# Eight matmuls of the ones matrix with itself at TensorE's beginning

## What is computed

```python
def rms_norm(x, g):
    y = x * lax.rsqrt(jnp.mean(x * x, axis=-1, keepdims=True) + RMS_EPS)
    return y * g
def swiglu(x, w1, w3, w2):
    return (jax.nn.silu(x @ w1) * (x @ w3)) @ w2

x = x + 0.5 * swiglu(rms_norm(x, g_ffn1), w1_ffn1, w3_ffn1, w2_ffn1)
...
x = x + concat(attention, gated_spatial_mix) @ w_out + b_out
x = x + 0.5 * swiglu(rms_norm(x, g_ffn2), w1_ffn2, w3_ffn2, w2_ffn2)
x = x + sigmoid(rms_norm(x, g_ple) @ w_ple_gate) * (ple @ w_ple_proj)
```

## Time and profile before

| | us |
|---|---|
| median of 3 executions | 979.13 |
| all of them | 979.13, 980.75, 979.12 |
| the profiled execution | 978.99 |
| its span, from the first instruction to the last | 977.2 |
| mean granted TensorE clock | 0.998 of full |
| busy: PE / DVE / ACT / POOL | 960.1 / 673.4 / 456.0 / 251.7 |

### The profile page before, as it was taken

One profiled execution on the slowest core, in us unless ns is written; L12 is line 12 of the kernel. 1 busy time (PEld: TensorE's weight loads), 2 busy tenths in 40 slices (PEclk: granted clock), 3 DMA queues, 4 the chain that ended last, 5 costly groups with the idle time before them and its releaser, 6 DMA issues.

```text
span 977.2 us, 19305 instructions
## 1 busy us (share of the span) xinstructions
PE 960.1 (98%) x7949; PEld 946.1 (97%) x7949; DVE 673.4 (69%) x1071; ACT 456.0 (47%) x746; POOL 251.7 (26%) x146
## 2 busy tenths in 40 slices
PE   7999999999999999999999999999999999999997
PEld 7999999999999999998899999999999999999997
DVE  6999567757668564467765399857766758855476
ACT  7555335533534444665444455534543443635243
POOL 0212211211111226422308411301221211114621
PEclk9999999999999999999999999999999999999999
DMA  8931524152143327321124693253324325235202
GB/s 240 172 88 55 161 66 119 46 163 78 53 131 108 98 76 206 82 65 45 44 60 125 129 173 97 64 143 97 98 81 115 98 61 144 66 98 163 88 22 88
DMA packets 190098, 100.33 MB, mean 103 GB/s; under 512 B 12986, under 2 KB 187412, under 8 KB 189996
## 3 DMA queue, kind: packets, MB, share of 16 engines
q1 hardware_dynamic: 176612, 90.27, 32.5%
q0 software_dynamic: 9360, 4.72, 3.9%
q10 hardware_dynamic: 4040, 4.12, 1.4%
HBM read 96.54 MB, written 3.59 MB: 102 GB/s over the span
## 4 chain that ended last, share of the span: by engine, by line
PE 86%; DVE 9%; issue 2%; ACT 1%; DMA 1%; SPq 0%; DVEq 0%
PE ps L1778 46%; PE ps L1858 34%; PE ps L2205 2%; PE ps L1814 1%; DVE w_lo L1350 1%; DMA x_rows<-in_x_prompt_dram 1%; PE ps L2079 1%; DVE xo_lo L1316 1%; PE ps L2108 1%; DVE w_lo L1476 0%; DVE tt L1275 0%; DVE w_raw L1339 0%; DVE tt L1494 0%; PE ps L1803 0%; DVE xo_raw L1293 0%
## 5 line engine op out<-in xcount | busy, mean ns | idle before, releaser
L1858 PE MATMUL ps<-xo_hi,w_hi 128*128 128x260 f32 x1008 | 284.2, 282 | 1.2 <-DVE ab L1373 1.2
L1858 PE MATMUL ps<-xo_lo,w_hi 128*128 128x260 f32 x1008 | 284.7, 282 | 0.0
L1858 PE MATMUL ps<-xo_hi,w_lo 128*128 128x260 f32 x1008 | 284.4, 282 | 0.0
L1778 PE MATMUL ps<-h_hi,w_hi 128*128 128x260 f32 x960 | 195.3, 285 | 1.0 <-issue 0.6
L1778 PE MATMUL ps<-h_hi,w_lo 128*128 128x260 f32 x960 | 193.0, 282 | 0.0
L1778 PE MATMUL ps<-h_lo,w_hi 128*128 128x260 f32 x960 | 192.9, 282 | 0.0
L1858 PEld LDWEIGHTS ps<-xo_hi,w_hi 128*128 128x128 f32 x1008 | 189.6, 188 | 1.3 <-issue 1.3
L1858 PEld LDWEIGHTS ps<-xo_hi,w_lo 128*128 128x128 f32 x1008 | 189.8, 188 | 0.0
L1858 PEld LDWEIGHTS ps<-xo_lo,w_hi 128*128 128x128 f32 x1008 | 189.7, 188 | 0.0
L1778 PEld LDWEIGHTS ps<-h_hi,w_hi 128*128 128x128 f32 x960 | 147.5, 188 | 2.5 <-issue 1.3
L1778 PEld LDWEIGHTS ps<-h_lo,w_hi 128*128 128x128 f32 x960 | 148.1, 188 | 0.0
(11 more groups left out here) (280 smaller groups left out, 1449.1 us busy)
## 6 DMA issues: line engine op xcount, KB each, us to landing
w_raw<-in_w_ffn_dram SPq DMA_DIRECT2D x88, 256.0 KB, 3.1
w_a<-in_w_ffn_dram SPq DMA_DIRECT2D x36, 512.0 KB, 4.8
w_raw<-in_w_ffn_dram SPq DMA_DIRECT2D x48, 384.0 KB, 3.3
w_raw<-in_w_ffn_dram SPq DMA_DIRECT2D x16, 512.0 KB, 6.0
w_raw<-in_w_in_dram SPq DMA_DIRECT2D x10, 512.0 KB, 4.0
w_lo<-in_w_ffn_dram POOLq DMA_DIRECT2D x9, 512.0 KB, 7.4
w_raw<-in_w_ple_gate_dram SPq DMA_DIRECT2D x8, 512.0 KB, 3.6
x_rows<-in_x_prompt_dram SPq DMA_DIRECT2D x8, 256.0 KB, 6.1
```

The source lines that it names most:

```text
L1778: ins = pe.matmul(ps[:, bank + step * h, 0:HALF], w[:, c, w0:w0 + P], m_[:, sk, h * HALF:(h + 1) * HALF], start=(first and n == 0), stop=( ...
L1858: ins = pe.matmul(ps[:, b, 0:Q], w[:, c, k * P:(k + 1) * P], m_[:, op, k, :], start=(first and k == 0 and n == 0), stop=(k == 3 and n == 2 ...
```

## The change

Between the wait for the constants and the wait for the gains, TensorE multiplies `ones` by `ones` eight times, into the first 128 columns of bank 0. Nothing waits for these matmuls and nothing reads their result; the first up tile begins this bank anew. No semaphore is added.

```diff
             pe.wait_ge(consts_ready, 4)
+            for _ in range(8):
+                pe.matmul(ps[:, 0, 0:P], ones[:], ones[:], start=True, stop=True)
             pe.wait_ge(gain_in, 16)
             pe.transpose(ps[:, 7, 0:KD], rows[0:KD, :], ident[0:KD, 0:KD]).then_inc(cols_turned, 1)
             pe.wait_ge(x_in[NB], 16)
```

## The result

The changed kernel takes 982.43 us (median of 22 executions, 980.32 to 983.87), the kernel before 979.76 (22 executions, 978.70 to 981.46): a ratio of 1.0022, 95% interval 1.0016 to 1.0028. Forecast was 979.0, within 978.2 to 980.4. So it is slower, by about as much as the bound of 0.2% that the prediction set. The profiled execution takes 982.27, its span is 980.2. Three executions among all runs (1036, 1436 and 1561 us, at a lower granted clock) are left out of every comparison.

What follows compares the result with a forecast made beforehand. TensorE was taken to bound the kernel (busy 98% of the span), except in the first 20 us, where the chain runs over other engines. 978.99 - 0.1 = 978.9, set at 979.0 for the runs' median; range 978.2 to 980.4.

Steps and rivals of the forecast that it cites:

- Cost of the added work and what it delays: TensorE's start: 16 records take 3.34 us, until 5.14; samples' transposes 0.54 later, hidden by waits and DVE's slack.
- The rise of the clock: First 14 us: TensorE reaches full clock about 6.8 instead of 13.6 us, within the left halves' transposes; gain 0.1 us.
- rival 1: At the start the clock stays at half until 10 or 13.6 us: 979.4 us, chance 0.20.
- if the 32 transposes all take 421: Sign of being wrong: all transposes of `x_rows` at the start still take 421 ns, the half-clock time.
- That a faster TensorE gains next to nothing there: Right halves' transposes save 1.5 us on TensorE, but DVE's and ACT's streams let only 0.1 through.
- The longer wait for `w_lo` at 20 us: TensorE's first up tile starts about 0.9 us sooner, so it waits longer than 0.43 us for the second's `w_lo`.
- a gain of 0.1 us: Copy of slice 0 comes at about 8.75 instead of 8.85 us, and 0.1 passes through the ACT stream.
- the second up tile begins at 20.05 instead of 20.15: Last step of the sum, near 20 us: TensorE's second up tile starts 0.1 us earlier, taken off 978.99.
- Rival 3: Half-clock stretch from 484.6 to 488.1 us goes away, saving 1.7: 977.4 us, chance 0.08; under 977.2, chance 0.03.
- a sign of being wrong: The prediction listed itself as wrong if the half-clock stretch at 485 us is gone.
- Rival 4: TensorE idles from 8.4 to 10.3 us, clock falls again, first up tile slow: 980.4, chance 0.05; over 981.1, chance 0.03.
- That the clock rises behind transposes alone: At 13.6 us the trace shows the clock rising after nothing but transposes, against a skill rule; the sum follows the trace.

Runs made afterwards that it cites:

- e1: The changed kernel run once more, with no further edit: 981.88 us, 1.0020 to the kernel before.
- e9: Kernel before plus two 128x512 ones matmuls at TensorE's beginning instead of the change's eight, so 8 instructions more: 980.24 us, 1.0006.
- e5: Changed kernel with 32 instructions fewer at TensorE's end, transposes there replaced by six fast matmuls, so the old program length: 980.30 us, 0.9999.
- e3: Kernel before with the eight ones matmuls at the end of TensorE's program instead of its beginning: 981.66 us, 1.0020.
- e2: Kernel before, unedited, loaded as a second program: 980.77 us, 1.0010.
- e6: Kernel before with transposes at TensorE's end replaced by six fast matmuls, 32 instructions fewer, no early ones matmuls: 979.93 us, 0.9995.

## Why the prediction was wrong

- *Cost of the added work and what it delays*: right in kind, short in size. The 16 records took 3.78 us where 3.34 were reckoned, so the gains' transpose came at 5.48 and not at 5.14. The left halves began at 6.23 (forecast 6.22) all the same, by luck: the clock rose earlier than chosen, and the samples' transposes took 0.69 us instead of 1.02. The cost stayed hidden behind loads and DVE's slack: copy of slice 0 at 8.74 (forecast 8.75), copy of slice 4 without idle time, second up tile at 20.03 (forecast 20.05).
- *The rise of the clock*: right in kind in the change's profile, full before the first transpose of `x_rows`, where I had chosen 6.8. In e1's profile of the same kernel *rival 1* (chance 0.20) came true instead, and with it the sign "if the 32 transposes all take 421". That a faster TensorE gains next to nothing there, since DVE's and ACT's streams set the end: right. The longer wait for `w_lo` at 20 us didn't come (0.43 before and now); TensorE spent the time inside the tile (0.21 of it waiting for `h_lo` at 15.36). The kernels with the early work and no slow loads agree: e9 1.0006 and e5 0.9999, each with an interval around no difference. They can't confirm a gain of 0.1 us.
- **The step that failed is the one that wasn't there.** The sum ended at 20 us: "the second up tile begins at 20.05 instead of 20.15", and the 957 us behind it were taken over unchanged. The prediction counted the 16 records by their run time and never as 32 more instructions of a program. What happened is that 384 KB loads take 0.3 us longer, which five places in the program can't hide (1.7 us). It isn't the early work: e3 has the eight at the far end and the same loss, e5 has them at the beginning and the old length and no loss.
- *Rival 3* spoke of the fall at 484.6 going away, at a gain of 1.7. It did go away in the change's profile, which was a sign of being wrong, and nothing was gained: the wait for `mix_lo` behind it absorbed it (1.6 against 2.8 us), and behind the longer idle time the clock fell, at full price. It fell there in all four profiles with a wait of 2.8 us and in none of the eleven with 1.3 to 1.6; that the idle time is the cause isn't shown. The rival's price was taken from the lost work alone, without asking what ends last behind it. The form changes without a change of program: the kernel before has the short fall at 484 in one profile and the long one in the other (e2), and the change has the one at 510 and, in e1, the short one near 486. So it is at least in part spread among executions; whether the change makes a dear form more frequent stays open.
- *Rival 4*, my only slower one, didn't occur: TensorE was idle for 2.02 us ahead of 10.22 and the transposes behind ran at 273 ns.
- That the clock rises behind transposes alone: the trace had said so and nothing speaks against it. In e6, with the old beginning, the left halves were at half rate and the right halves already at full.

## What to carry to other kernels

A change that adds instructions is to be tested against the same instructions at a place where they can't matter, before anything is read into a difference of a few tenths of a per cent. Where a kernel's loads arrive just in time, list those places: they turn 0.3 us of landing time into 1.7 us. And the price of a clock fall is what its end delays: 3.4 us at half rate were nearly free ahead of a wait that could take them up and cost over 1 us behind it, and 6.7 us ahead of the same wait cost 1.4 as well.

## What the runs showed of the hardware

- The landing time of 384 KB loads stepped from 3.1 to 3.3 us up to 3.5 to 3.6 when TensorE's program grew by 12 instructions or more, wherever they stood. 8 more, 32 fewer or 32 on POOL left it, and loads of 256 KB stayed at 3.1 in the change. By what way the length acts is open: device memory placement wasn't told apart.
- Single executions of the kernel before spread from 978.7 to 982.1. In the same program the clock fell near 484 us for 3.4 us or for 6.7 (before, e2), and in another at 511 or near 486 (change, e1).
- The first rise differs in the same program too: the change's 32 transposes all took 273 ns (median) in one profile and 421 in another.
- Ahead of the first recorded change of the clock its column misled: PEclk read 1.00 from 1 to 5 us, where the ones matmuls took 421 ns.
